# Layer 0's adaLN vectors split between the opening and the even projections; neighbourhood values in split products; early loads moved

## What is computed

```python
mod_l = silu(c) @ ada_w[layer] + ada_b[layer]           # 6 * 1024, latent tokens
mod_c = silu(c_ctx) @ ada_w[layer] + ada_b[layer]       # context tokens
sh1, sc1, g1, sh2, sc2, g2 = split(mod_l, 6)            # vectors 0 to 5
h = rmsnorm(x) * g * (1 + sc1) + sh1                    # into the projections: vectors 0 and 1
x = x + g1 * (mixer(h) @ w_out)                         # vector 2
x = x + g2 * (square(relu(modulate(x, sh2, sc2) @ w1)) @ w2)   # vectors 3, 4 and 5
# neighbourhood attention, layer 1: per grid row, 8 rows x 64 columns of keys plus the context
p = softmax(q @ k.T * scale + bias, masked);  o = p @ v
```

## Time and profile before

| | |
|---|---|
| timed runs | 3883.83, 3893.90, 3894.23 us, median 3893.9 |
| profiled execution | 3889.35 us, its span 3887.3 us |
| busy share of the span | PE 92%, DVE 51%, ACT 33%, POOL 5% |
| TensorE's mean granted clock | 0.953 of full speed |
| DMA | 364 MB by SP's queue, mean 94 GB/s |
| a load or store of 1 MB of h, issue to landing | 5.4 and 5.3 us (median) |
| a 2 MB load of ada_w, issue to landing | 8.9 us (median of 12) |

### The profile page before, as it was taken

The page is one execution under the profiler, slowest core; times in us unless marked ns, Lnnn a source line. Parts: engine busy times, 40 slices in busy tenths (PEclk is TensorE's granted clock), DMA queues, the critical chain, the costliest instruction groups (busy, mean ns, idle before and its releaser), DMA issues. The chain is left out here.

```text
span 3887.3 us, 47332 instructions
## 1 busy us (share of the span) xinstructions
PE 3588.0 (92%) x17690; PEld 2866.6 (74%) x17690; DVE 2001.3 (51%) x2876; ACT 1284.8 (33%) x2279; POOL 175.1 (5%) x178
## 2 busy tenths in 40 slices
PE   9798888897899999999989889799899899999999
PEld 2586665786788888888867768577677678888887
DVE  2556554886664444444455455588554363333333
ACT  2453333664431101111125445466433341111111
POOL 0210010000110000000001000000000020000000
PEclk9898899998999999999999989799899899999999
DMA  8335563423321222221214444533244311111112
GB/s 315 122 141 185 156 160 85 104 62 92 90 83 51 69 69 69 57 65 50 69 54 152 150 144 140 124 74 73 50 102 92 114 50 46 49 49 48 52 54 65
DMA packets 431073, 366.47 MB, mean 94 GB/s; under 512 B 103350, under 2 KB 374086, under 8 KB 425798
## 3 DMA queue, kind: packets, MB, share of 16 engines
q1 hardware_dynamic: 430917, 364.42, 32.6%
HBM read 276.67 MB, written 87.69 MB: 94 GB/s over the span
## 5 line engine op out<-in xcount | busy, mean ns | idle before, releaser
L2157 DVE SCALAR_TENSOR_TENSOR xT<-ps,mods,xT 128x1024 f32<-128x1024 f32 x192 | 189.4, 1014 | 420.5 <-PE ps L2371 420.5
L2371 PE MATMUL ps<-e_gh,e_w2h 128*128 128x512 f32 x1280 | 355.6, 375 | 6.0 <-DVE e_w2l L2616 3.6
L2371 PE MATMUL ps<-e_gl,e_w2h 128*128 128x512 f32 x1280 | 351.7, 372 | 0.0
L2371 PE MATMUL ps<-e_gh,e_w2l 128*128 128x512 f32 x1280 | 351.2, 372 | 0.0
L2666 DVE TENSOR_TENSOR e_plain<-e_plain 128x1280 f32<-128x1280 f32 (+1 forms) x64 | 87.0, 1359 | 481.8 <-ACT e_plain L2531 481.8
L2371 PE MATMUL ps<-e_hl,e_w1h 128*128 128x512 f32 (+1 forms) x1200 | 327.2, 370 | 0.0
L2371 PE MATMUL ps<-e_hh,e_w1h 128*128 128x512 f32 (+1 forms) x1200 | 327.1, 370 | 0.0
L2371 PE MATMUL ps<-e_hh,e_w1l 128*128 128x512 f32 (+1 forms) x1200 | 327.1, 370 | 0.0
L2531 ACT ACTIVATE e_plain<-ps 128x1280 f32<-128x1280 f32 (+1 forms) x64 | 72.7, 1135 | 757.7 <-PE ps L2371 753.7
L2371 PEld LDWEIGHTS ps<-e_gh,e_w2h 128*128 128x128 f32 x1280 | 224.2, 189 | 55.2 <-DVE e_gl L2670 8.0
L2371 PEld LDWEIGHTS ps<-e_gl,e_w2h 128*128 128x128 f32 x1280 | 225.4, 189 | 43.3
(11 more groups left out here) (375 smaller groups left out, 7437.6 us busy)
## 6 DMA issues: line engine op xcount, KB each, us to landing
e_raw<-in_mlp_w SPq DMA_DIRECT2D x64, 512.0 KB, 4.2
e_raw<-in_mlp_w SPq DMA_DIRECT2D x128, 256.0 KB, 3.0
aw<-in_ada_w SPq DMA_DIRECT2D x12, 2048.0 KB, 8.9
rstd<-in_ada_w SPq DMA_DIRECT2D x64, 384.0 KB, 3.4
e_raw<-in_w_out SPq DMA_DIRECT2D x40, 512.0 KB, 3.9
qkC<-pc_stage SPq DMA_DIRECT2D x72, 192.0 KB, 2.7
hT<-pb_hb SPq DMA_DIRECT2D x10, 1024.0 KB, 5.4
pa_hb<-hT SPq DMA_DIRECT2D x10, 1024.0 KB, 5.3
```

Of the source, the lines that this page charges most:

```text
L2157: ins = k.nc.vector.scalar_tensor_tensor(out=x, in0=ps, scalar=k.mods[:, layer, gate, bass.ds(n, 1), w], in1=x, op0=ALU.mult, op1=ALU.add)
L2371: mm = pe.matmul(k.ps[:, SB * (e % 2) + b, 0:n], w[:, e % 2, f], m[:, f, c0:c0 + n], start=(f == 0 and x == 0), stop=(f == nf - 1 and x == 2))
```

## The change

1. **Opening.** `N_HALVES` falls from 12 to 4: only vectors 0 and 1 are computed there. The list of steps has all remaining token tiles right after the first half. Squares, their sums, roots and reciprocals go by chunks of 512, 512 and 256 tokens, at steps 0 to 2; the sums over partitions take two accumulated products per chunk.
2. **`project` with `vectors`.** Phase `pb` makes vectors 2 and 3, `pa` vectors 4 and 5. `ada_w` comes in slices of 128 x 512 (256 KB) through the `raw` slots when the weights are cut. For each slice VectorE multiplies it by a column of silu(c) or silu(c_ctx) and adds it to an accumulator (two operations); after eight slices TensorE sums the accumulator over partitions by one-column fp32 products with `ones`, and VectorE adds the bias. That makes 8 groups of 8 slices, two slices per job over four jobs of a group (six jobs apart in `pb`, four in `pa`). `pa` gets three PSUM banks for products instead of four.
3. **`attend`.** `split` becomes an argument of its own; `ad` now has it true. `ahead_of.load(sp)` moves from the start of the first pair to its end, in `ab` and `ac`. `stacked_loader` issues q and k before v.

The diff, cut to its core:

```diff
@@ opening @@
-        N_HALVES = 6 * D_MODEL // HALF
+        N_HALVES = OPENING_VECTORS * D_MODEL // HALF
-        steps = [("x", t) for t in range(XB)]
-        for n in range(N_HALVES):
-            steps += [("ada", n)] + [("x", t) for t in (XB + 2 * n, XB + 2 * n + 1) if t < NT]
-
-        X_DONE, SUM_AT = 3, 8
+        steps = [("x", t) for t in range(XB)] + [("ada", 0)] + [("x", t) for t in range(XB, NT)] + [("ada", n) for n in range(1, N_HALVES)]
+        PAIRS = KT // 2
+        squared_at, summed_at = {0: (0,), 1: (1, 2)}, {1: (0,), 2: (1, 2)}
...
+                def sums(c):
+                    if c == 0:
+                        pe.wait_ge(s.xcpA, NT)
+                        pe.wait_ge(s.xcpD, NT)
+                    pe.wait_ge(s.acc, (c + 1) * (PAIRS - 1))
+                    for a in range(2):
+                        mm = pe.matmul(k.ps[:, TB + c, 0:chunks[c][1]], k.ones[:], both(c)[:, a], start=(a == 0), stop=(a == 1))
@@ project @@
-    RAW, LAG, MB, TB = 6, 2, 4, 4
+    RAW, LAG, TB, GC = 6, 2, 4, 512
+    MB, AB, ACCS = (3, 3, 2) if vectors and not keeps_h else (4, 7, 1)
+    NW, NG = len(slices), len(vectors) * D_MODEL // GC
+    PERIOD, FIRST = (N - U - 2) // NG if NG else 0, U
...
+    def slices_at(n):
+
+        g, y = (n - FIRST) // PERIOD, (n - FIRST) % PERIOD
+        if n < FIRST or g >= NG:
+            return range(0)
+        busy = PERIOD - 2 * (2 - ACCS)
+        return range(g * KT + min(KT, y * KT // busy), g * KT + min(KT, (y + 1) * KT // busy))
...
+                def fetch_vectors(a):
+                    x = NW + a
+                    if a < RAW:
+                        sp.wait_ge(s.wlo, x - RAW + 1)
+                    else:
+                        sp.wait_ge(s.aacc, 2 * (a - RAW + 1))
+                    sp.dma_start(raw[:, x % RAW], a_dram[a_group[a // KT], a % KT]).then_inc(wr[x % RAW], 16)
...
+                def vector_sums(g):
+                    pe.wait_ge(s.aacc, 2 * (g + 1) * KT)
+                    if g:
+                        pe.wait_ge(s.modd, g)
+                    for c in range(GC // P):
+                        for w in range(2):
+                            mm = pe.matmul(k.ps[:, AB, 2 * c + w:2 * c + w + 1], a_acc[g % ACCS][:, w, c * P:(c + 1) * P], k.ones[:, 0:1],
+                                           start=True, stop=True)
+                    mm.then_inc(s.asum, 1)
...
+                def vector_part(a):
+                    x, g, f = NW + a, a // KT, a % KT
+                    dve.wait_ge(wr[x % RAW], 16 * (x // RAW + 1))
+                    if f:
+                        dve.wait_ge(s.aacc, 2 * a)
+                    elif g >= ACCS:
+                        dve.wait_ge(s.asum, g - ACCS + 1)
+                    for w in range(2):
+                        here = a_acc[g % ACCS][:, w]
+                        if f == 0:
+                            part = nc.vector.tensor_scalar(here, raw[:, x % RAW], k.sil2[:, f, w:w + 1], None, ALU.mult)
+                        else:
+                            part = nc.vector.scalar_tensor_tensor(out=here, in0=raw[:, x % RAW], scalar=k.sil2[:, f, w:w + 1],
+                                                                  in1=here, op0=ALU.mult, op1=ALU.add)
+                        part.then_inc(s.aacc, 1)
...
                     if keeps_h and n == first_of[t] and t + 1 < NT:
                         split_h(t + 1)
                         inverse(t + 2)
+                    for a in slices_at(n) if NG else ():
+                        vector_part(a)
+                    for g in group_after(n, 4) if NG else ():
+                        vector_sum(g)
@@ attend @@
-    split = parts == "three"
+    three = parts == "three"
...
-                        if ahead_of is not None:
-                            ahead_of.load(sp)
...
                     if first and beside is not None:
                         beside.last_store(s, sp)
+                    if first and ahead_of is not None:
+                        ahead_of.load(sp)
@@ stacked_loader @@
+        if q_sb is not None:
+            keys(sp, h, kh, q_sb, k_sb, q_top, k_top, near, far)
         if v_sb is not None:
             sp.dma_start(v_sb, v_dram.rearrange("(t p) d -> p t d", p=P)[:, :, bass.ds(vh * v_width, v_width)]).then_inc(far, 16)
-        if q_sb is None:
-            return
@@ trunk @@
-            Unit(0, 512, v=512, v_dst=k.vA)], keeps_h=True)
+            Unit(0, 512, v=512, v_dst=k.vA)], keeps_h=True, vectors=(2, 3))
...
-            Unit(512, 512, 8, ins["diff_k_g"][0], 1.0, True, k.qkA, 8)], keeps_h=False, ahead_of=ahead_b)
+            Unit(512, 512, 8, ins["diff_k_g"][0], 1.0, True, k.qkA, 8)], keeps_h=False, ahead_of=ahead_b, vectors=(4, 5))
...
-               "two", HD, k.mix[1], 512, bias=bias_loader(k), ahead=ahead_d)
+               "two", True, HD, k.mix[1], 512, bias=bias_loader(k), ahead=ahead_d)
```

More of the change, by code:

```diff
@@ L42 @@
 SBUF_END = 229344
+VECTORS, OPENING_VECTORS = 6, 2
 SLICE = 4
@@ L325, in turn_rows @@
                     mm.then_inc(s.colT, 1)
-                def sums():
-                    pe.wait_ge(s.acc, KT)
-                    for c, (c0, n) in enumerate(chunks):
-                        mm = pe.matmul(k.ps[:, TB + c, 0:n], k.ones[:], acc[:, c0:c0 + n], start=True, stop=True)
+                def sums(c):
[5 more added lines that the diff above has]
+                        mm = pe.matmul(k.ps[:, TB + c, 0:chunks[c][1]], k.ones[:], both(c)[:, a], start=(a == 0), stop=(a == 1))
                     mm.then_inc(s.sum, 1)
@@ L339, in _ @@
                             turn_rows(n - 1)
-                        if n == SUM_AT:
-                            sums()
+                        for c in summed_at.get(n, ()):
+                            sums(c)
                 turn_rows(N_HALVES - 1)
@@ L374, in _ @@
                     else:
-                        if X_DONE <= n < X_DONE + KT // 2:
-                            squares(2 * (n - X_DONE))
-                            squares(2 * (n - X_DONE) + 1)
+                        for c in squared_at.get(n, ()):
+                            for g in range(PAIRS):
+                                squares(c, g)
                         rows_out(n)
-                        if n == SUM_AT:
-                            roots()
+                        for c in summed_at.get(n, ()):
+                            roots(c)
             @block.vector
@@ L510, in project @@
         w_dram = w_in.rearrange("(f p) n -> f p n", p=P)
+        if NG:
+            free = nc.alloc_sbuf_tensor_at(f"{name}_aacc", [P, 2, GC], F32, offset=rope_at)
+            a_acc = [free[:], k.rstd[:, 0:2 * GC].rearrange("p (w n) -> p w n", w=2)][0:ACCS]
+            a_dram = k.ins["ada_w"][layer].rearrange("(k p) (g n) -> g k p n", p=P, n=GC)
+            a_group = [j * D_MODEL // GC + y for j in vectors for y in range(D_MODEL // GC)]
         assert ahead_of is None or nc.sbuf_base <= ahead_of.end
@@ L569, in _ @@
                         store_v(n)
+                    if n == FIRST - 1:
+                        for a in range(min(RAW, NG * KT)):
+                            fetch_vectors(a)
+                    for a in slices_at(n - 1) if NG else ():
+                        if a + RAW < NG * KT:
+                            fetch_vectors(a + RAW)
                 for m in rest:
@@ L617, in _ @@
                         turn(m)
+                    for g in group_after(n, 3) if NG else ():
+                        vector_sums(g)
                 for m in rest:
                     turn(m)
+                for n in range(N, N + 3):
+                    for g in group_after(n, 3) if NG else ():
+                        vector_sums(g)
             @block.scalar
@@ L1341, in steps_of_head, with attend @@
     return out, blocks
-def attend(k, name, pieces, heads, load_head, parts, v_width, mix, mix_col, sink=None, bias=None, beside=None, ahead=None, ahead_of=None):
+def attend(k, name, pieces, heads, load_head, parts, split, v_width, mix, mix_col, sink=None, bias=None, beside=None, ahead=None, ahead_of=None):
     nc = k.nc
@@ L1408, in sb @@
             return st.enter_context(nc.sbuf_tensor(f"{name}_{nm}", shape, dt))
-        D = MLA_QK if split else HD
-        if split:
+        D = MLA_QK if three else HD
+        if three:
             q_sb, k_sb = [[sb(f"{a}{p}", [D + 1, 2, TOK], F32R) for p in range(2)] for a in "qk"]
```

99 lines of the change are left out of this document (62 added, 37 removed).

## The result

The changed kernel takes 3870.1 us (median of four runs, 3868.0 to 3870.9), the kernel before 3893.6 in runs on the same chip (3883.8 to 3894.2). The ratio on record is 0.9945, with a 95% interval of 0.9929 to 0.9960: 0.55% faster (the two medians alone give 0.9940). The forecast was 3860.0, range 3832 to 3882. So the sign and the range held; between the two profiles the gain is 18.5 us, six tenths of the 30.5 that I had worked out. The profiled execution took 3870.9 us (span 3868.8, granted clock 0.947; before: 3889.35, 3887.3 and 0.953), and both profiles are single executions.

What follows compares the result with a forecast made beforehand. It took TensorE's own order of work to set the end in nearly every phase, with VectorE having room. Terms -49 + 29 + 14.5 - 9 - 16 = -30.5 gave 3858.9 on the profile, forecast as 3860.0 us, range 3832 to 3882.

Steps and rivals of the forecast that it cites:

- The opening: Opening: eight of twelve half vectors leave TensorE (-58.3), three things come back; -49 us in all.
- the landing of the second half: Opening: its load, issued behind the last two token tiles, lands at 36.5 us and makes TensorE wait; +5.3 us.
- rival C: A gain fails to come: loads sharing queues in the opening, ab's wait moved on, or VectorE-bound ad; 3869 to 3876, chance 0.11.
- the cold half: Opening: after the gap the clock is at its lower level, so the next half runs slower; +1.6 us.
- the sums: Opening: column sums of squares become twelve matmul instructions where six took 2.42 us; +2.4 us.
- pb: Phase pb: VectorE's slices delay the low part TensorE waits for, stalling eight tiles, plus column sums; +29 us.
- The stall of 3.7 a tile: pb: slices 2.9 plus turns with GpSimd 2.4, less 1.6 us free; 3.1 in a group's first tile, 27 over eight tiles.
- rival B: pb: stalls drop the clock, losing 1.6 to 3 us in each of eight tiles; +19, 3878 us, chance 0.13.
- rival D: pb and pa: stalls return before the clock has risen, so tiles with slices run at 1.2 GHz; about +180, 4040 us, chance 0.04.
- pa: Phase pa: slices make VectorE set the pace of 16 jobs, 7.23 us each instead of 6.37; +14.5 us.
- ab: Phase ab: moving the next phase's loads removes TensorE's 7.2 us wait for keys and the low clock after it; -9 us.
- ad: Phase ad: three products of the new kind replace two fp32 instructions per values step, the added work hidden; -16 us.

Runs made afterwards that it cites:

- e3_aw: The changed kernel with the load of the second ada_w half issued ahead of the last two token tiles instead of behind them; 3863.3 us, ratio 0.9936.
- e8_spread: The changed kernel with pb's slices mid-tile, next-phase loads at the last pair, the second half's load earlier, and one vector moved from pa to pb; 3836.5 us.
- e2_last: The changed kernel with the loads for the next phase issued at the start of the last pair of heads in ab and ac; 3855.5 us, ratio 0.9914.
- e6_ad_alone: The kernel before with only the split of the values products in ad; 3879.5 us, ratio 0.9977.
- e0: A phase of the kernel, not a run, its code untouched by the change; 1097.7 us in the kernel before, 1103.4 in the changed kernel.
- e4_novec: The changed kernel without the four adaLN vectors of pb and pa, a constant in their places, so output differs from the reference; 3820.4 us, ratio 0.9827.
- e7_lock: The changed kernel with GpSimd's product for the next tile in pb held back until that VectorE job's slices are done; 3856.9 us, ratio 0.9917.
- e1_mid: The changed kernel with pb's 32 slices in the second and third job of each tile instead of the first four of six; 3843.5 us, ratio 0.9883.

## Why the prediction was right or wrong

**The opening: right, 3.7 short.** The failed term is the landing of the second half. I had put 3.1 MB at 395 GB/s, the rate of a stretch with one large load in flight, plus 2 us, at 36.5; it landed at 39.9. Of these 3.4 us, 1.4 are the start: SP issued the last token tiles at 27.73 and not at 26.31, since the first half took 9.79 and not 8.60. The other 2.0 are the load, 12.2 us instead of 10.2. From 26 to 40 us the core moved 3.99 MB, 0.8 more than x8, x9 and this half, at 399 GB/s in the last 4 us; so part of the next halves came in beside it, which is rival C's sharing on a small scale (argued from the bytes, not tested). No row of before shows the 2 us until the first bytes by themselves. TensorE turned its last tile at 34.4 and not at 31.2, and so the wait is 5.5 for my 5.3, but the landing alone sets the end. The rest of the term held: the cold half (+1.5 for +1.6), the sums (1.99 and 2.85 where six took 2.42, so +2.4 for +2.4). e3_aw shows that this wait was a matter of order, not of bytes.

**pb: right mechanism, +33.9 for +29, by two errors that partly cancel.** The stall of 3.7 a tile came out at 3.24, since GpSimd's share was 2.1 and not 2.4 (5.06 less 2.93) and the slack 1.8 and not 1.6 (5.06 less 3.24), while the slices cost 2.93 for my 2.9; in the tiles with sums it is 0.95 beside 1.9 of sums, 2.8 in all for my 3.1. Waits of 16.4 and sums of 7.6 make 24.0, where I had 27 and 1.8, 28.8: 4.8 less. What I had left out of the forecast, and given to rival B, was the clock behind the stalls. B did happen, at half its price: 10.6 us by TensorE's busy time, not 19, because the clock fell in four tiles and not in eight; 2.6 us in each of the four lies inside my 1.6 to 3. The other four stalls, of 0.9 to 1.1 us, left it at 1.00. The granted clock is 0.82 across one such stall and 0.77 in a worse stretch, and 0.99 over the 30 us before the first of these, so rival D's condition (it stays down from one stall to the next) was never met. My sentence "with a granted clock of 1.00" for these tiles was wrong.

**pa: right, +11.8 for +14.5.** VectorE is the bound, with a job every 7.08 us for my 7.23: 12 jobs times 0.15 is 1.8 of the 2.7. The slices had the price I gave them (2.93 for 2.9); the mis-sized term is the rest of the job, 4.15 and not 4.3. I had also read the 1.18 us of idle at 336.25 as VectorE being late. The kernel before has five jobs 5.50 us apart with 1.18 us idle each, up to 352.75, so the early jobs simply come faster; the sum does not rest on it. e8_spread shows the bound by taking half of it away.

**ab: wrong, +0.4 for -9.** The step that failed is "with nothing in front of them". There is something in front of them: the second store of bias tables, issued after the first pair (L1265), 5.95 us itself and with 12.70 for the load behind it. I had read the queue at the place the loads left and only the next pair's loads at the place they went to. The prediction had the outcome as rival C, "the wait in ab moved on", with a share of 0.11. It did move, by one pair, and grew from 7.2 to 9.1 (to 10.2 and more in the other kernels). e2_last shows that the 9 us were to be had, from the start of the last pair.

**ad: the size right, -17.3 for -16, the cause half seen.** I read the phase as running near a clock of 1.00, where the earlier trace rows has 0.95; that changes no term. I had worked out the products saved and called everything else hidden. The split does save its products, but in e6_ad_alone two thirds of the gain are lost: 8.2 us in waits for keys and some 4 in slower products. What was missing is the question what is late next: with 0.4 us of wait for ad_k before, the keys had next to no slack, and heads that are some 2 us shorter (17.9 over eight) had to wait for them. That the price of this step came out right is in part luck: I had the edit that made it come out, but for another phase. The other edit of the change, keys ahead of values, removed that wait before I could see it.

**The phases outside the change.** e0's +5.7 is within the differences of single executions. pc's -6.2 is not: it is 237.4 to 239.4 in the four kernels with the old opening and 229.7 to 232.2 in the eight with the new one, in e4_novec too, where pb and pa do nothing new. So it is neither the vectors, the split, the loader nor the later loads, all of which leave it at 238; it goes with the opening, whose code ends two thousand microseconds earlier. In pc 3.6 of the 6.2 us are in TensorE's waits for ScalarE's `pc_stage` (13.8 us in twelve waits before, 10.2 in eight after), whose releaser in turn is the store of heads, and 2.0 in its waits for `pc_wl` (17.4 and 15.4). Why a different opening should change that stays open.

**The sum.** The forecast was 10 us low, 12 on the profiles. Without the ab step it would have been within 1 of the median and within 3 of the profile, but only because pb's clock (10.6 more), its stalls (4.8 less) and pa (2.7 less) partly cancel inside it.

## What to carry to other kernels

Work added to an engine with room costs by its place in that engine's queue: the same 32 slices cost pb 35 us in front of an operation that TensorE waits for, and 7 us one job further on. When a load is moved, read the queue where it arrives as closely as where it left, for stores like the one of bias tables here above all; and when work is taken out of a loop, look at the slack of what is loaded for its next turn. A stall on TensorE is to be counted with the clock behind it, here two thirds of the waits once more, all of it behind the four long ones.

## What I had not expected of the hardware

- Four stalls of 2.7 to 3.2 us within 100 us of dense work cost 10.6 us of TensorE time in slower products: the granted clock over the 7 us behind them is 0.76, 0.76, 0.76 and 0.51. Four stalls of 0.9 to 1.1 us in the same phase leave it at 1.00. The length alone does not decide: in e7_lock three stalls of 1.7 us are followed by 1.00, 0.76 and 1.00. Without stalls the phase has 0.93 (e1_mid).
- The same two operations, with the same recorded starts 0.03 us apart, end in two ways: low part 0.68 us and GpSimd's product 2.97 (before, 200.86 and 200.83), or low part 2.90 and product 2.39 (e8_spread, 158.56 and 158.53). One of them waits for the whole of the other, and the starts in the record do not say which.
- The load issued right behind the store of bias tables (1.9 MB) sits in SP's queue for 12 to 13 us (12.70, 12.24, and 13.22 before), in three kernels and behind two different stores, and what SP issues next is late by as much. From 500 to 572 us of the changed kernel 15797 of 18545 packets are under 512 B; that the small packets are the reason was not tested.
